# First attention of a two-layer trunk: each short query tile placed between long ones of its head, and the raw output copied out of PSUM by ScalarE

## The reference

```
def attend(qb, kk, vv):
    s = jnp.einsum('bqhmd,bkhmd->bhmqk', qb, kk).astype(f32) * scale
    p = jax.nn.softmax(s, axis=-1)
    a = p[:, :, 0] - lam * p[:, :, 1]
    return jnp.einsum('bhqk,bkhe->bqhe', a.astype(vv.dtype), vv)

def finish(o):
    o = _rmsnorm(o, sub_g) * (1 - lam_init)
    return o.reshape(o.shape[0], o.shape[1], -1) @ wo

k_all = jnp.concatenate([k, kc], axis=1)      # 1024 image + 256 context keys
o  = attend(each block of 128 image queries, k_all, v_all)
yc = finish(attend(qc, kc, vc))               # context queries see 256 keys only
```

## Time and profile before

| | |
|---|---|
| median of 3 runs | 3064.97 us |
| the profiled execution | 3065.03 us, span of its instructions 3063.2 us |
| TensorE busy over the span | 2743.3 us (90%) |
| VectorE, ScalarE, GpSimd busy | 1299.9, 781.0, 673.5 us |
| first attention | from 532.1 us (first scores) to 976.7 us (end of the last put) |
| one head in it | 54.45 us |
| TensorE, VectorE, ScalarE busy in one head (597.0 to 651.5 us) | 51.25, 48.16, 38.78 us |

### The profile page before, as it was taken

The page is one execution under the profiler, slowest core; times in us unless marked ns, Lnnn a source line. Parts: engine busy times, 40 slices in busy tenths (PEclk is TensorE's granted clock), DMA queues, the critical chain, the costliest instruction groups (busy, mean ns, idle before and its releaser), DMA issues.

```text
span 3063.2 us, 38668 instructions
## 1 busy us (share of the span) xinstructions
PE 2743.3 (90%) x15193; PEld 1491.9 (49%) x15193; DVE 1299.9 (42%) x2420; ACT 781.0 (25%) x1743; POOL 673.5 (22%) x915
## 2 busy tenths in 40 slices
PE   6999999999998996999999769979999779987973
PEld 2444433888886553333333234468875433432321
DVE  3544310898986454111111164479974520100104
ACT  2211100777765110000000053146651000000001
POOL 2555300455553220100000034500002100000001
PEclk9999999999999996999999989989999789998996
DMA  6344467424322227999999575253322298999996
GB/s 251 111 100 140 163 252 234 96 52 92 65 67 109 96 89 324 379 385 420 405 381 427 246 290 134 74 126 56 68 71 97 103 417 370 384 398 424 397 401 241
DMA packets 199412, 684.33 MB, mean 223 GB/s; under 512 B 26688, under 2 KB 122096, under 8 KB 166208
## 3 DMA queue, kind: packets, MB, share of 16 engines
q1 hardware_dynamic: 101344, 583.01, 51.1%
q10 hardware_dynamic: 84896, 61.07, 6.3%
q0 software_dynamic: 12992, 37.77, 3.1%
HBM read 607.81 MB, written 83.43 MB: 226 GB/s over the span
## 4 chain that ended last, share of the span: by engine, by line
PE 74%; DMA 13%; DVE 7%; issue 2%; ACT 1%; POOL 1%; SPq 1%; POOLq 0%; ACTq 0%; DVEq 0%
PE psum L443 17%; PE psum L1760 14%; DMA moe_ring<-in_e_w 11%; PE psum L1318 8%; PE psum L1775 8%; PE psum L990 4%; PE psum L942 4%; PE psum L1117 3%; PE psum L1104 2%; PE psum L947 2%; PE psum L1145 2%; PE psum L410 1%; PE psum L1737 1%; PE psum L1307 1%; PE psum L1935 1%
## 5 line engine op out<-in xcount | busy, mean ns | idle before, releaser
L1760 PE MATMUL psum<-moe_ring,moe_xT 128*32 128x512 f32 (+2 forms) x3744 | 610.9, 617 | 53.2 <-DMA moe_ring<-in_e_w 51.0
L443 PE MATMUL psum<-qkv_w,act_hT 128*128 128x512 f32 x1376 | 612.3, 598 | 1.5 <-ACT act_hT L544 1.3
L1760 PEld LDWEIGHTS psum<-moe_ring,moe_xT 128*32 128x32 f32 (+2 forms) x3744 | 206.0, 124 | 427.0 <-issue 424.1
L443 PEld LDWEIGHTS psum<-qkv_w,act_hT 128*128 128x128 f32 x1376 | 256.8, 192 | 309.3 <-issue 307.0
L1775 PE MATMUL psum<-moe_ring,moe_hT 128*32 128x512 f32 (+2 forms) x1872 | 301.5, 605 | 17.1 <-DMA moe_ring<-in_e_w 16.3
L1844 DVE TENSOR_TENSOR moe_hh<-psum,moe_sg 128x512 f32<-128x512 f32 x42 | 29.1, 692 | 624.5 <-PE psum L1760 624.5
L1318 PE MATMUL psum<-wo,out_oT 128*128 128x512 f32 x576 | 255.2, 598 | 1.8 <-DVEq L1365 1.4
L1049 DVE TENSOR_REDUCE att_nmax<-psum 128x1 f32<-128x1280 f32 (+1 forms) x160 | 204.1, 1276 | 28.4 <-PE psum L942 27.1
L942 PE MATMUL psum<-att_kT,att_q 128*128 128x512 f32 (+1 forms) x832 | 197.4, 369 | 9.9 <-ACTq L173 5.1
L1005 ACT ACTIVATE att_prob<-psum,att_nmax 128x1280 f32<-128x1280 f32 (+1 forms) x160 | 185.3, 1158 | 56.3 <-DVE att_nmax L1049 52.9
L1775 PEld LDWEIGHTS psum<-moe_ring,moe_hT 128*32 128x32 f32 (+2 forms) x1872 | 98.9, 122 | 188.1 <-issue 184.3
(11 more groups left out here) (247 smaller groups left out, 3329.0 us busy)
## 6 DMA issues: line engine op xcount, KB each, us to landing
moe_ring<-in_e_w SPq DMA_DIRECT2D x192, 2048.0 KB, 21.3
ada_w<-in_ada_w SPq DMA_DIRECT2D x48, 1024.0 KB, 6.6
qk_d<-qkv_stg ACTq DMA_DIRECT2D x112, 256.0 KB, 2.8
att_q<-qk_d SPq DMA_DIRECT2D x32, 640.0 KB, 12.2
att_q<-qk_d SPq DMA_DIRECT2D x64, 256.0 KB, 5.2
qkv_w<-in_a_wqkv SPq DMA_DIRECT2D x6, 2048.0 KB, 9.7
att_kT<-qk_d SPq DMA_DIRECT2D x32, 320.0 KB, 5.8
prep_y<-y_d SPq DMA_DIRECT2D x10, 1024.0 KB, 7.5
```

The source lines that it names most:

```text
L443: ins = nc.tensor.matmul(psum[:, u.par, :], hT[:, k, u.t * P:(u.t + 1) * P], qw[:, u.C % 2, k], start=(k == 0), stop=(k == KD - 1))
L1760: ins = nc.tensor.matmul(psum[part, bank, :], xT[:, 4 * half + k, part], ring[:, CHUNK[l][r, half] % RING, k, bank * DE:(bank + 1) * DE], ...
```

## The change

```
-    UNITS0 = [(h, t) for h in range(KD) for t in range(TA)]
+    UNITS0 = [(h, t) for h in range(KD) for t in (0, 1, 2, TX, 3, 4, 5, TX + 1, 6, 7)]
     def full_before(n):
-        return n // TA * TX + min(n % TA, TX)
+        return sum(t < TX for h, t in UNITS0[:n])
...
+        def take_output(n):
+            act.wait_ge(s_av, n + 1)
+            if n >= 2:
+                act.wait_ge(s_on, n - 1)
+            nc.scalar.activation(raw[:, n % 2], psum[:, 7, 0:P], ACT.Copy).then_inc(s_raw, 1)
+
         def square(n):
...
             expo(n + 1, 0)
             if n:
+                take_output(n - 1)
                 square(n - 1)
             act.wait_ge(s_turn[0], n + 1)
...
+        take_output(N0 - 1)
         square(N0 - 1)
...
-        def copy_output(n):
-            dve.wait_ge(s_av, n + 1)
-            if n >= 2:
-                dve.wait_ge(s_on, n - 1)
-            nc.vector.tensor_copy(raw[:, n % 2], psum[:, 7, 0:P]).then_inc(s_raw, 1)
...
             weigh(n)
-            if n:
-                copy_output(n - 1)
             peak(n + 1, 1)
...
-        copy_output(N0 - 1)
```

## The result

The changed kernel takes 3079.91 us (median of 5 runs, 3069.81 to 3081.95) where the kernel before takes 3064.97 (5 runs, 3060.97 to 3067.51). The ratio is 1.0045, its 95% interval 1.0028 to 1.0062: slower by 0.3 to 0.6%, 3081 being forecast. Two later comparisons, each with fresh runs of both kernels, gave 1.0053 (1.0037 to 1.0069) and 1.0046 (1.0032 to 1.0060). The profiled execution after is the slowest of the five: 3081.95 us, span 3080.0, 16.8 more than the span before, where the medians differ by 14.9.

A forecast was written before the change was run, and what follows sets the result against it. TensorE bounds the first attention on the mean, a three-engine chain the lighter turns before long units. Seven heads +11.4 and the last head +4.7 make +16.1 us on 3065.03: 3081 us, range 3070 to 3093.

The forecast's parts named there:

- What bounds a turn: First attention, between successive units' first transposes: TensorE's work sets 5.84 us; with less work, a three-engine chain sets 5.24.
- the chain: VectorE's maximum, ScalarE's exp, VectorE's reciprocal and mix, TensorE's next transposes, serving a long next unit: 5.24 us in sum.
- The order of the units: First attention: short units standing singly between long ones make a head 56.08 us against 54.45, +1.63; seven heads +11.4.
- the turn ahead of a short unit: Tile 2 or 5 of a head: TensorE's full work plus 0.06 us for transposes after a gap, 5.90 us.
- The last head: End of the first attention, now closing with long tiles 6 and 7: 56.84 us against 52.18, +4.7 us.
- The copy on ScalarE: 80 raw-output copies leave VectorE, 0.41 us each on ScalarE, covered by its idle time: zero in 79 units, +0.1 at the end.
- Rival A: First attention: long neighbours fill a short unit's gaps and only TensorE's work is left; -31 us, 3034; chance 0.08.
- B: Chain-set turns: the lighter VectorE shortens each by 0.3 us, leaving +6.2 us, 3071, so no change; chance 0.07.
- C: ScalarE's new wait for the product delays its exps: 13.5 us on top, 3095, or 3114 in all turns; chance 0.05.
- Rival D: Gaps in short units' turns drop TensorE's clock to 1.2 GHz, one turn each: 48 us on top, about 3129; chance 0.02.

## Why the prediction was right, and where not

- **What bounds a turn.** Right. The steps of the chain were read as 0.20, 1.53, 1.45, 0.46 and 1.60 us from tile 6's turn, and the new short turns show the same. The kernels with the shortened chain show that it is a cause: the turns moved with two of its links.
- **The order of the units**, forecast +1.63 us a head, measured +1.46. The term that was off is the turn ahead of a short unit: 5.90 forecast, 5.81 measured. I had added 0.06 for transposes after a gap and kept 5.84 for the rest; the product ran 0.1 shorter there, as it had in the turn of tile 0 (5.82), the row that I should have gone by.
- **The last head**, forecast +4.7, measured +4.1 without its slow turn. Its last two turns took 4.89 and 7.17 against 4.99 and 7.43; the others are the term above.
- **The copy on ScalarE**, forecast zero in 79 units. Right in the new order: 55.89 us a head with VectorE's copy, 55.91 with ScalarE's. In the old order, of which the forecast said only that VectorE's copy had been on the path there, it cost 0.11 us a head. The price, 0.37 us by the nearest row, was 0.27: the row that I took reads its scale from memory, the copy does not, and VectorE takes 0.28. The Trainium skill, Advanced Engine Details and Errata (The Read-Write Bubble), places ScalarE nearer to PSUM; I had set the rows against it, and the like comparison shows the two engines 15 ns apart.
- **Rival A** (gaps filled by long neighbours) fell with the turns at 5.24, **B** with the unchanged chain, **C** with the copy's cover: ScalarE's copy of blocks 0 to 3 starts 0.64 us into the turn in the median and 0.70 at most, as before, turns with a fall apart.
- **Rival D**, the clock, had 0.02 and one fall for each short turn. Its mechanism took place behind 8 of 64 short turns, for 1.6 us in most, so its time of 3129 was far off and the forecast should instead have carried a term of some 3 us. The Trainium skill's warning in TensorE: Matmul & The Clock Gate (A second HAM failure mode), that many small idles make the clock swing, fits these traces better than my reading of the one head in which gaps of 0.94 and 1.12 us had left it alone.
- **The total.** 3081 forecast, 3079.91 measured. It is partly luck: the order was worth 14.3 us in the profiled execution instead of 16.1, and the lowered clock, not in the sum, added 5.1 (3.2 of it behind short units), while other phases gave back 2.6. The median on which the forecast is measured is of executions without a trace, so how many falls they had isn't known.

## What to carry to other kernels

In a pipeline through several engines, a light unit saves time only if the chain that serves its neighbour is light too: look, in the profile of the present order, for a light turn with a heavy one behind it, and take its length as the price of each place where the two meet. Put the light units side by side, which here gave 0.3%, rather than spread them. Look at the granted clock too when gaps are added to TensorE's turns: here some 3 us of the loss were falls of the clock, and cheap work in the gap went with their absence in three traces.

## What the runs showed of the hardware

- A copy of 128 by 128 fp32 values from PSUM takes ScalarE 0.27 us with constants and 0.37 with a scale read from memory; VectorE takes 0.28.
- Transposes of the identity, issued in a row, cost TensorE 0.11 us each (four in 0.44), and nine of them ahead of the waiting scores did not lengthen the turn.
- TensorE's granted clock fell to its lower level behind turns in which it was busy for 3.5 of 5.2 us and idle for 1.10 and 0.62 us: behind 8 of 64 such turns, and behind none of 48 with at most 0.67 and 0.62 us idle. A fall cost 1.6 us in seven cases and 0.5 in one. In the old order a turn with a single gap of 1.42 to 1.45 us had none behind it in 7 cases.
